# A hybrid streaming encoder step on one core: expert-row pairs moved inside the retrievals, queries beside the last norm, four one-hot buffers, first-key one-hots made in one operation per token

## The reference, cut to what matters

```python
h = rmsnorm(x); x += (sig(ga)*conv_branch(h) + sig(gb)*retention_branch(h)) @ w_out   # T = 512 + 8*16 tokens, D = 1024
h = rmsnorm(x)
q = (h @ w_q).reshape(T, 8, 2, 128)
s = einsum('thpd,pkd->thpk', q, sub_keys)          # 128 keys per side
sv, si = top_k(s, 16)                              # per side
cand = sv[:, :, 0, :, None] + sv[:, :, 1, None, :] # 256 pairs
ts, tp = top_k(cand, 16); e = cidx[tp]; g = softmax(ts)
a = gelu(einsum('thkd,td->thk', u_tab[e], h))      # 128 experts for each token
x += einsum('thk,thkd->td', g * a, v_tab[e])
y = rmsnorm_final(x)
```

## Time and profile before

| what | value |
|---|---|
| median of 3 runs | 2468.25 us (2466.16 to 2470.9) |
| the profiled execution | 2473.17 us, of which the span is 2471.4 us |
| PE busy | 2318.6 us, 94% of the span |
| DVE busy | 1624.5 us, 66% |
| POOL busy | 766.6 us, 31% |
| ACT busy | 369.1 us, 15% |
| one `turn` (L941) on DVE | 1242 ns, 128 of them |
| transfers | 726.80 MB, mean 294 GB/s |

### The profile page before, as it was taken

The page is one execution under the profiler, slowest core; times in us unless marked ns, Lnnn a source line. Parts: engine busy times, 40 slices in busy tenths (PEclk is TensorE's granted clock), DMA queues, the critical chain, the costliest instruction groups (busy, mean ns, idle before and its releaser), DMA issues.

```text
span 2471.4 us, 27566 instructions
## 1 busy us (share of the span) xinstructions
PE 2318.6 (94%) x9545; PEld 1589.2 (64%) x9545; DVE 1624.5 (66%) x2850; ACT 369.1 (15%) x667; POOL 766.6 (31%) x606
## 2 busy tenths in 40 slices
PE   6899889899999999999999997999999999999997
PEld 5889779799997865655565654666644444444443
DVE  4466565567753088769879878888565655656556
ACT  3212212122231101111111111323200000000001
POOL 4212111123350002551651640101044544545440
PEclk9999889999999999999999998999999999999999
DMA  4998988998860326897996994767799999999994
GB/s 156 291 320 263 293 260 284 307 305 301 287 223 18 124 93 237 328 412 292 352 412 248 408 412 141 223 223 225 245 392 369 392 401 384 402 391 382 413 394 159
DMA packets 324118, 726.80 MB, mean 294 GB/s; under 512 B 30112, under 2 KB 179360, under 8 KB 324000
## 3 DMA queue, kind: packets, MB, share of 16 engines
q1 hardware_dynamic: 199776, 431.28, 49.9%
q0 software_dynamic: 73728, 268.47, 27.8%
q10 hardware_dynamic: 50496, 25.59, 3.4%
HBM read 595.65 MB, written 129.57 MB: 293 GB/s over the span
## 4 chain that ended last, share of the span: by engine, by line
PE 54%; issue 16%; DVE 12%; DMA 11%; POOL 6%; ACT 1%; SPq 0%; POOLq 0%; ACTq 0%; DVEq 0%
PE ps L1642 27%; DMA b<-in_peer_v,b 9%; PE ps L1597 6%; PE ps L1567 6%; PE ps L1612 3%; POOL b L615 3%; PE ps L1376 3%; PE ps L1377 3%; PE ps L1378 3%; POOL b L580 3%; DVE ps L1279 1%; DVE b L1188 1%; DVE b L1183 1%; DVE b L1192 1%; PE ps L1397 1%
## 5 line engine op out<-in xcount | busy, mean ns | idle before, releaser
L1597 PE MATMUL ps<-b,b 128*128 128x384 f32 x2048 | 681.3, 494 | 23.0 <-ACT b L816 23.0
L1642 PE MATMUL ps<-b,b 128*128 128x512 f32 x1536 | 661.2, 594 | 2.0 <-ACT b L816 2.0
L1597 PEld LDWEIGHTS ps<-b,b 128*128 128x128 f32 x2048 | 394.7, 194 | 295.4 <-issue 40.4
L615 POOL DMA_INDIRECT b<-u_rows,b x256 | 246.7, 964 | 972.5 <-DVE b L1258 728.9
L1642 PEld LDWEIGHTS ps<-b,b 128*128 128x128 f32 x1536 | 293.1, 191 | 369.9 <-issue 366.6
L1376 PE MATMUL ps<-b,b 128*128 128x320 f32 x1152 | 367.8, 319 | 5.0 <-ACT b L643 4.5
L1377 PE MATMUL ps<-b,b 128*128 128x320 f32 x1152 | 361.3, 314 | 0.0
L1378 PE MATMUL ps<-b,b 128*128 128x320 f32 x1152 | 361.1, 313 | 0.0
L615 POOL DMA_INDIRECT b<-in_peer_v,b x256 | 312.2, 1220 | 140.2 <-DVE ps L1279 79.8
L1279 DVE SCALAR_TENSOR_TENSOR ps<-b,b,ps 128x1024 f32<-128x1024 f32 x252 | 324.5, 1288 | 45.8 <-DMA b<-in_peer_v,b 24.7
L580 POOL TENSOR_TENSOR b<-b,b 128x1024 fp32r<-128x1024 f32 x80 | 194.9, 2440 | 513.7 <-ACT b L628 509.3
(11 more groups left out here) (148 smaller groups left out, 1795.2 us busy)
## 6 DMA issues: line engine op xcount, KB each, us to landing
b<-in_u_t SPq DMA_DIRECT2D x256, 512.0 KB, 6.4
u_rows<-b SPq DMA_DIRECT2D x512, 128.0 KB, 4.1
b<-in_peer_v SPq DMA_DIRECT2D x128, 512.0 KB, 8.2
b<-in_w_in SPq DMA_DIRECT2D x72, 512.0 KB, 5.7
acts<-b SPq DMA_DIRECT2D x128, 192.0 KB, 7.9
gates<-b ACTq DMA_DIRECT2D x12, 2048.0 KB, 7.7
b<-gates SPq DMA_DIRECT2D x32, 768.0 KB, 9.0
b<-acts SPq DMA_DIRECT2D x32, 768.0 KB, 15.2
```

The lines of the kernel that those rows point to most:

```text
L615: nc.gpsimd.indirect_dma_start(slots[n % SLOTS][:, :], None, u_rows if kind == "u" else v_rows, bass.IndirectOffsetOnAxis(ap=row_id[:, r_ ...
L1597: last = nc.tensor.matmul(ps[:, 2 + e % UP_BANKS, 0:TD], w[:, k * P:(k + 1) * P], h2[:, k, SD:T], start=(k == 0), stop=(k == KT - 1))
L1642: last = nc.tensor.matmul(ps[:, 2 + 2 * i + dh, :], p32[:, e % GROUP, i * P:(i + 1) * P], w[:, dh * 512:(dh + 1) * 512], start=(e == 0), s ...
```

## The change

The change has seven parts.

1. The transposing ring becomes two `u_in` and three `u_turned` buffers (five as before). Each load now waits for the turn two tiles earlier and not three; each turn waits for the store of three tiles earlier and not two.
2. The order of turns on DVE: before the first head's k rotation there are 2 turns and not 6 (8 behind it and 2 in the first `scores`); in the rounds of heads 1 to 3 `prompt_state` comes before the turn that preceded it, and the turns behind it move by one. The last head's order stays.
3. The first two query tiles of the first 256 tokens are done before the last tile's norm transposes and the row transposes. The squares of the second norm are dumped in `h_row` and not in PSUM; the retrieval constants are asked for earlier.
4. Nine pair steps lie inside each of retrievals 1 to 4, and six between two retrievals (54 in all, as before); `retrieval(1)` comes behind the first dots. `EXP_AT`, `SCORES_AT`, `PICKT_AT` and `pair_at` follow.
5. The gates start at e = 102 and not 101. The one-hot ring has four places.
6. `eq1` goes: for each token one `tensor_scalar` (equal, then times the weight) writes `ew`; `eq2` is made as before.
7. The last four down tiles are multiplied token tile by token tile, and `final_sums(i)` waits for its own token tile.

```diff
-EXP_AT = {1: 4, 2: 35, 3: 66, 4: 96}
-SCORES_AT = {2: 6, 3: 52, 4: 82}
-PICKT_AT = {2: 41, 3: 72, 4: 101}
-PAIRS_AT = (8, 39, 70)
-GATE_AT = 101
+EXP_AT = {1: 12, 2: 40, 3: 67, 4: 95}
+SCORES_AT = {2: 8, 3: 49, 4: 77}
+PICKT_AT = {2: 46, 3: 74, 4: 101}
+GATE_AT = 102
-GAP = 18
+INSIDE = 9
+GAP = 6
+CYCLE = INSIDE + GAP
+HOTS = 4
 def pair_at(b):
-    gap = b // GAP
-    return PAIRS_AT[gap] + b % GAP * 26 // 25 if gap < 3 else GATE_AT + 2 + 4 * (b - 3 * GAP)
+    if b >= NPAIR_R:
+        return GATE_AT + 2 + 4 * (b - NPAIR_R)
+    turn, i = b // CYCLE, b % CYCLE
+    e = 27.4 * turn + (-3.3 + 2.35 * (i + 0.3) if i < INSIDE else 17.4 + 1.04 * (i - INSIDE))
+    return max(0, int(e))
...
             def turn_in(m, r=0, per=0, first=False):
-                if not (first and m < 3):
-                    sp.wait_ge(turned, r * per + (m - 2))
-                sp.dma_start(u_in[m % 3], ...)
+                if not (first and m < 2):
+                    sp.wait_ge(turned, r * per + (m - 1))
+                sp.dma_start(u_in[m % 2], ...)
                 if not (first and m < 2):
                     turn_out(m - 2, r, per)
...
             turn(0, 6)
             rotate_q(0)
-            turn(6, 6)
+            turn(6, 2)
             rotate_k(0)
-            turn(12, 6)
+            turn(8, 8)
...
                 rotate_k(h)
+                prompt_state(g, first)
                 turn(5, 1, h, PER_HEAD)
-                prompt_state(g, first)
-                turn(6, 1, h, PER_HEAD)
                 for s in range(STREAMS):
                     stream_state(g, s)
-                    turn(7 + s, 1, h, PER_HEAD)
-                outputs(g, lambda: turn(15, 1, h, PER_HEAD))
+                    turn(6 + s, 1, h, PER_HEAD)
+                outputs(g, lambda: turn(14, 2, h, PER_HEAD))
...
-                line.then(nc.vector.tensor_tensor(eq1[:, :, :], keys, each(k1T[:, tok]), ALU.is_equal))
-                line.then(nc.vector.tensor_tensor(eq2[:, par, :, :], keys, each(k2T[:, tok]), ALU.is_equal))
-                nc.vector.tensor_tensor(ew[:, par, :, :], eq1[:, :, :], each(wT[:, tok]),
-                                        ALU.mult).then_inc(onehot_ready, 1)
+                for t in range(BLK):
+                    at_ = blk_ * BLK + t
+                    nc.vector.tensor_scalar(ew[:, par, t, :], iotaK[:, :], k1T[:, at_:at_ + 1], wT[:, at_:at_ + 1],
+                                            ALU.is_equal, ALU.mult)
+                nc.vector.tensor_tensor(eq2[:, par, :, :], keys, each(k2T[:, tok]),
+                                        ALU.is_equal).then_inc(onehot_ready, 1)
...
             retrieval(0)
-            retrieval(1)
             for r_ in range(AHEAD * PAIR):
                 dot(r_)
-            for tt in range(NS, TT):
-                ... 18 pair steps ...
-                retrieval(tt)
+            for tt in range(1, TT):
+                retrieval(tt, next_pair)
+                for i in range(GAP if tt < TT - 1 else 0):
+                    next_pair()
+                    if i == 1 and tt >= NS:
+                        picks_out(tt)
...
+            pe.wait_ge(h_ready, 2 * TT + 2 * NS)
             for i in range(A_WQ):
                 query(i, slice(0, SD))
+                if i == 1:
+                    norm_step(TT)
+                    ... the row transposes of the first two tiles ...
...
+            for e in range(NKEY - GROUP):
                 ... as before ...
+            for i in range(ND):
+                for e in range(NKEY - GROUP, NKEY):
+                    if i == 0:
+                        plain_tile(2 * A_WQ + NKEY + e)
+                        pe.wait_ge(p_ready, e + 1)
+                    last = down(e, i)
+                last.then_inc(sums_done, 1)
```

More of the change, by code:

```diff
@@ L515, in _ @@
                 if i == 0:
-                    for b in range(2):
-                        sp.wait_ge(u_stored[b], 64 * (NKEY // 2))
+                    for b in range(3):
+                        sp.wait_ge(u_stored[b], 64 * ((NKEY + 2 - b) // 3))
                     for tt in range(TT):
@@ L647, in norm_row @@
                 n = which * TT + tt
-                dump = junk[:, :] if which == 2 else ps[:, 2:4, :].rearrange("p a b -> p (a b)")
+                dump = (ps[:, 2:4, :].rearrange("p a b -> p (a b)"), h_row[:, 0, :], junk[:, :])[which]
                 nc.scalar.activation(dump, x[:, tt, :], ACT.Square,
@@ L954, in scores @@
                 dve.wait_ge(tabs_loaded, g * 48 + 48)
+                if isinstance(g, int) and g == 0:
+                    turn(16, 2)
                 for j in range(PT + 1):
@@ L1171, in settle, with top_sixteen @@
                 line.mark(nc.vector.memset(nothing[:, 0:1], 0.0))
-            def top_sixteen(rows, less, values, places):
+            def top_sixteen(rows, less, values, places, between):
                 every = list(enumerate(zip(rows, less)))
@@ L1184, in top_sixteen @@
                 line.then(last)
+                between()
                 settle()
@@ L1193, in top_sixteen, with retrieval @@
                 line.then(last)
-            def retrieval(tt):
+            def retrieval(tt, between=lambda: None):
                 dve.wait_ge(s_done, tt + 1)
                 sc = [ps[:, 4 + s // 4, (s % 4) * NKEY:(s % 4 + 1) * NKEY] for s in range(SIDES)]
-                top_sixteen(sc, [rest[:, s, :] for s in range(SIDES)], val, idx)
+                top_sixteen(sc, [rest[:, s, :] for s in range(SIDES)], val, idx, between)
                 nc.vector.tensor_copy(idx_f[:, :, :], idx[:, :, :]).then_inc(s_used, 1)
                 dve.wait_ge(s_used, tt + 1)
+                between()
                 vv = val[:, :, :].rearrange("p (h s) k -> p h s k", s=2)
@@ L1205, in retrieval @@
                     vv[:, :, 1, :].unsqueeze(2).broadcast_to([P, PH, TOPK, TOPK]), ALU.add))
-                top_sixteen([cand[:, h, :] for h in range(PH)], [cand2[:, h, :] for h in range(PH)], ts, tp)
+                top_sixteen([cand[:, h, :] for h in range(PH)], [cand2[:, h, :] for h in range(PH)], ts, tp, between)
+                between()
                 line.then(nc.vector.tensor_copy(mx[:, 0, :], ts[:, :, 0]))
@@ L1328, in _ @@
                 if blk_ % 8 == 6:
[L1329 to L1330 removed]
+                    next_pair()
+            b = taken[0]
             for e in range(NKEY):
```

92 lines of the change are left out of this document (47 added, 45 removed).

## The result

The changed kernel takes 2366.64 us (median of 4 runs, 2364.64 to 2372.28), the kernel before 2469.57 us beside it (4 runs): a ratio of 0.9588, 95% interval 0.9568 to 0.9609, or 103 us less. Forecast were 97 us less and 2371 us, with a range of 2351 to 2420. The profiled execution took 2364.64 us, its span 2362.8 us; that is 108.5 us under the span before, which had been an execution 3.6 us above the median of its four runs.

The account below looks back on a forecast made before the run. PE's work plus its pauses bounds the kernel, DVE mattering only where work stands late in its order. Terms 24.3 + 5 + 65 + 5.5 − 1 = 98.8, rounded down to 97, took the 2468.25 us median to 2371; range 2351 to 2420.

Parts of the forecast that it names:

- input products: First stage: moved copies, earlier k rotation and third output buffer together save 24.3 us, bounds 14 less 4 to 44.
- two moved copies and first head's: Input products: prompt-state copy ahead of a waiting turn saves 14.4 us in two heads, 2.4 in the first.
- first rotated k: Input products: rotating k four turns earlier ends PE's 8.78 us pause, but later scores wait; 5 us saved.
- last head, third output buffer: Input products, last head: order kept, only the third output buffer can help; 2.5 of 9.97 us saved.
- last norm: Before the up products: two queries fill PE's 4.7 us standstill and the slow transposes; 5 us saved (0 to 6.3).
- up products and gates: Up products through the pause before down products: 771.6 us against 836.5, a gain of 65 (30 to 72).
- tail: After the last down matmul: one token tile remains; 7.1 us saved, 1 to 3 lost at v tile, net 5.5.
- turns waiting over 5 us for `in_u_t` with PE behind them: Input products: a stated sign that would show the prediction wrong, DVE's turns waiting over 5 us for loads.
- the turns bind at two inputs: Rival, input products: nothing won there, time 2395 us; chance 0.12 shared with one-hots at their bad bound.
- 758.4 us of PE work: Up products and gates: PE's own work at full pace, against windows adding up to 836.5 us.
- 5 us left for a late exponent: Up products: 5 us allowed for a late exponent or late rows in the first cycle.
- 31.0 us, under 34.9: Gates: DVE's eight blocks with a pair step take 31.0 us, PE's matching work 34.9.

Follow-up runs that it names:

- control: The changed kernel run once more with nothing altered; 2369.21 us, ratio 0.9582 to the kernel before.
- e_best: Changed kernel with the prompt state's copy moved further ahead in DVE's order, and first stream states ahead of turns in the last head; 2368.22 us.
- e_ring2: Changed kernel with two one-hot buffers again in place of four, the new operation kept; 2394.06 us.
- e_oldop: Changed kernel with the three old tensor_tensor operations for a block of one-hots again, the ring of four kept; 2376.91 us.
- e_normtail: Changed kernel with all queries behind the last norm's tiles again and the last four down tiles in their old order; 2382.15 us.
- e_best2: e_best with the last gate store split and the store the last Gelu waits for issued before the gate loads; 2361.94 us.
- e_both: Changed kernel with both the old three one-hot operations and two one-hot buffers again; 2402.35 us.

## Why the prediction was right, step by step

The forecast was 97 us, from a sum of 98.8. The two medians differ by 102.9. The profiled spans differ by 108.5, since the one before lies 3.6 us above its median and the one after 2.0 below. By these profiles:

| term | forecast | profile | undone alone |
|---|---|---|---|
| input products | 24.3 | 25.9 (22.8 in the control) | |
| two moved copies and first head's | 16.8 | 17.3 of waits | 14.8 of waits, 15.8 in time |
| first rotated k | 5 | 5.5 (2.7 in the control) | 4.0 of waits, 2.5 in time |
| last head, third output buffer | 2.5 | 1.0 | nothing there, 5.7 in the first head |
| last norm | 5 | 5.4 | 6.5 |
| up products and gates | 65 | 70.1 | 31.4 and 32.3 |
| down products | −1 | 0 | |
| tail | 5.5 | 7.1 | 7.2 |

The copies are the waits of 35.1 us less 16.8, without the last head's 9.97 − 8.97 = 1.0; the first rotated k is 8.8 − 3.3, in the control 8.8 − 3.2 − 2.9. The terms of the profile column add up to 108.5, so the forecast was short by 9.7 there, more than half of it (5.1) in the up products and gates.

**Input products.** Right in sum and in most terms. The step that failed is "The last head's 9.97 us keeps its order; only the third output buffer can help": it doesn't help there, and what it is worth, 5 to 7 us, lies in the first head, where I had given it nothing. The sum came out because one miss covered the other. That the turn would wait for the load where it had waited for the store was right; that this changes little was right for PE but not for DVE. Without the one long wait near 59 us that every profile has, the turns waited 158.3 us for stores and 1.3 for loads before, and 135.2 for loads after. One sign of being wrong did appear, turns waiting over 5 us for `in_u_t` with PE behind them: up to 7.4 us, in the last head. The kernel before had waits of up to 7.2 us for stores in that place, so it cost no more than before. The rival "the turns bind at two inputs" was wrong in its price: two inputs and three outputs are the better split. The remaining 16.8 us are not a matter of where the copy stands (`e_best`).

**Up products and gates.** The count of 758.4 us of PE work and the 8.2 us pause before the down products were the whole of it: 543.2 + 205.3 + 17.9 = 766.4, for 758.4 + 8.2 = 766.6. (The pause itself was 7.3, and 0.7 stood at a one-hot block.) That all 43.3 us of pauses and slow clock in the gates would go was right; that the clock comes back with the pauses was in this sum, though not in the later expectation for `e_ring2`. The 5 us left for a late exponent were not needed. The share of the transfers came to 0.96, not 0.92, and stalled nothing. The 0.25 us for a `tensor_scalar` were right as a pace (0.256), though one lasts 0.345 us; had the full length counted, 8 × (8 × 0.345 + 1.26) + 4.9 − 34.9 = 2.2 us would have been missing in each period. What the sum did not need, and what I had not said, is how the gain divides: most of the gates' gain hangs on the ring and not on the operation. Had only the operation been changed, the sum would have been 21 us too large, and the statement "31.0 us, under 34.9" alone would not have shown it: a mean that fits still stalls where a pair step falls between two blocks.

The Trainium skill, page "VectorE: DVE Perf Modes", section on the TRN2 errata, gave an estimate of 214 / 0.96 = 223 ns for such an operation by its fixed cost and its two columns a cycle. The page states that fixed cost for the length of a single operation. The trace has 345 ns in length, 55% above the estimate, and 256 ns from start to start, 15% above it. The direction agrees: at the 0.52 ns a column of the earlier trace rows, 128 columns are 67 of the 345 ns. The page's advice against short operations did not decide here: in `e_oldop` the three long ones cost 5.2 us more.

**Tail and down products.** The 7.1 us saved were right; the 1 to 3 us lost at the last v tile were not there. The lower clock behind the pause, for which the sum took 1 us, cost as much before as after, 1.7 and 1.6 us (a mean clock of 0.80 and 0.82 in the first 8.7 us). PE has no wait in the last 50 us of the down products, and `e_normtail` shows no time hidden in them. The last norm's step was right.

## What to carry to other kernels

When two engines work at nearly the same pace and one of them has a long step to put in now and then, look at the longest interval between two deliveries and not at the mean: here a ring of four bought 21 to 27 us, and one-hots of 3.37 us a block in place of 3.85 bought 5 to 11. The ring bridges the long step and does nothing for a mean that is too long. A wait for a transfer in an engine's order delays whatever stands behind it; moving one dependent forward pays until the next dependent takes its place, and then only the transfer or its place in its queue is left. And a pause of PE can cost more than its length: price the slower stretch behind it too. In `e_best2`, 4.2 us taken off a pause gave 2.3 more in the stage behind it.

## What the runs showed of the hardware

- Of six waits of 2.7 us on PE (`e_ring2`) two were followed by a stretch at the lower of the two clock levels, a mean of 0.80 in the next 8.7 us, and four were not; of six waits of 3.7 us (`e_both`) five were. Behind 3.1 us in front of the down products the clock was 1.00 in the next 8.7 us, behind 7.3 us 0.72 (`e_best`) and 0.82 (the changed kernel), but in the kernel before it was 0.80 behind 2.0 us there; so the length of the pause alone does not tell.
- Waits at the first keys, scores and stream steps differ from program to program in the same code, and the input products with them (709.8 to 719.2 us); the up products and gates behind them repeat to 0.1 us.
- A 128-column `tensor_scalar` with two column operands lasts 345 ns and starts every 256 ns; beside the 24 gathers that POOL issued, none of the 384 lasted over 471 ns.
- 543 us at a transfer share of 0.96 and 352 GB/s left PE without a pause; the share alone is no sign of a bound.
